# The last slot of a dense group: its eight narrow products first, then its wide ones tile by tile

## The chip, the cores and the metric

The kernel runs on one core of a Trainium2 chip. The metric is device time in microseconds (us) of one execution; the median of three runs is compared. Times inside the kernel come from one further execution, taken by the hardware profiler. Engines are named as the profile names them: PE (TensorE, matmuls), PEld (its weight loads), DVE (VectorE), ACT (ScalarE), POOL (GpSimd), SP (SyncE, which issues most DMAs).

## The reference

Two transformer blocks on 256 tokens of width 2048, in f32, with a final norm after each. What matters here is the order of the dense products:

```
first block:   p = rms_norm(x) @ w_in                      # 2048 -> 6000
               h = x + concat(rwkv7(p), sparse_attention(p)) @ w_mix_out
               h = h + cross_attention(rms_norm(h), rms_norm(mem))     # q, k, v, o
               h = h + square(relu(rms_norm(h) @ w_up)) @ w_down       # 2048 -> 8192 -> 2048
second block:  z = gelu(n @ a_w_in); u, v = split(z)                   # 2048 -> 2 x 4096
               h = h + gate * ((u * mix_tokens(rms_norm(v))) @ a_w_out)
               g, v = split(conv3(n @ ffn_w_up))                       # 2048 -> 2 x 5632
               h = h + gate * ((silu(g) * v) @ ffn_w_down)
```

## The kernel before

**Slots.** All dense weights come as one stream of 872 slots. A slot holds 256 rows by 512 columns of a weight matrix (512 KB) and lands by DMA in one of four ring places of `raw`. ACT copies it, rounded, to `whi` (L1933), DVE subtracts the two to `wlo` (L2282), and PE multiplies both. Semaphores keep the order: `hi_done` and `lo_done` count the two halves of a slot, and `slot_used`, raised by PE behind the last product that needs a slot, lets ACT write the ring place again.

**Wide and narrow products.** An operand is split in the same way, into a high part in columns 0 to 255 and a low part in columns 256 to 511 of `x`. A *wide* product multiplies `whi` with both (512 columns, L2742). A *narrow* one multiplies `wlo` with the high part alone (256 columns, L2746). Both add into one PSUM bank.

**Groups.** A dense group is 512 output columns: eight slots deep, four tiles of 128 columns wide, each tile in a bank of its own (two sets of four banks in turn). Each slot has two chunks `c` of 128 rows, so a slot is 8 wide and 8 narrow products. There are 64 such groups, all issued by `group()`: 12 in the first projection `w_in` (the last of them with three tiles), 4 in `mix_out`, 1 each for `k` and `q`, 16 in the first MLP (`mlp`), 8 in `a_uo`, and 22 in the conv FFN. The others, the down projections above all, go through `group_by_token` or `group_one_sum` and aren't touched.

Within a group, in `w_in` a slot's narrow products stand directly behind its wide ones. Elsewhere they stand in pairs: behind the wide ones of every second slot come the 16 narrow ones of both. The slot before the last has its narrow products alone. The last slot goes tile by tile: two narrow and two wide products of tile 0, then of tile 1, and so on, so that tiles are complete one after the other. `tile_done` tells of the first three, `slot_used` of the last.

**Asides.** Ahead of each slot's products a group may issue other PE work, `aside(g, s)`, with its own waits: index scores, `norm_k_t` (L1032), `bonus_t` (L1074) and `turn_t` (L1085 to L1089) of the mixer during `w_in`, `spread` (L2908) of the norm's factors in the first MLP group, `mixing` (L1802) in `a_uo`.

**Emptying a tile.** ACT's `half` (`hl`, L1940) waits for the tile and copies its upper 256 columns out of PSUM; DVE's `add` (L2307) adds the lower half to it and raises `evac_done`; further steps of the stage follow. `schedule()` puts the emptying of tile t on ACT and DVE behind the split of the t-th slot after the group's end, in one fixed order with the splits and with other work (L538, the ReLU of the index scores, stands on ACT behind the `half` of tile 0 of three groups in `w_in`). PE waits in some asides until all four tiles of a group are emptied (`evacuated(n)`: `evac_done` at 8 + 4n), or for a named step such as `rl2` or `rl5`, the ReLUs.

Of the kernel before, what the change touches and what calls it, by code (L numbers as in the profile page):

```python
# [1440 lines left out]
def build(nc, A, out):  # L1441
# [93 lines left out]
    L, n, g = {}, 0, 0  # L1535
# [1198 lines left out]
    def _(pe):  # L2734
        pe.sem_inc(slot_used, RING)

        def group(lin, i, g, x, ready, aside=None, tiles=4):

            p0, n = lin.ends[g] - lin.lens[g], lin.lens[g]

            def wide(s, c, t, stop=False):
                return pe.matmul(ps[:, lin.bank(g, t), :], whi[:, (p0 + s) % RING, c * 512 + t * P:c * 512 + (t + 1) * P],  # L2742
                                 x[:, 2 * s + c, :], start=s + c == 0, stop=stop)

            def narrow(s, c, t):
                return pe.matmul(ps[:, lin.bank(g, t), 0:T], wlo[:, (p0 + s) % RING, c * 512 + t * P:c * 512 + (t + 1) * P],  # L2746
                                 x[:, 2 * s + c, 0:T], start=False, stop=False)

            def narrows(s):
                pe.wait_ge(lo_done, lin.slot(i, p0 + s) + 1 + RING)  # L2750
                for c in range(2):
                    for t in range(tiles):
                        ins = narrow(s, c, t)
                ins.then_inc(slot_used, 1)

            for s in range(n - 1):
                if aside:
                    aside(g, s)
                begins = lin is L["w_in"] and (i, g, s) == (0, 0, 0)
                pe.wait_ge(*(hi_half, 1) if begins else (hi_done, lin.slot(i, p0 + s) + 1))  # L2760
                for c in range(2):
                    if begins and c:
                        pe.wait_ge(hi_done, 1)
                    if ready:
                        pe.wait_ge(ready[0], ready[1] + 2 * s + c + 1)
                    for t in range(tiles):
                        if s + c == 0:
                            pe.wait_ge(evac_done, lin.tile(i, g, t) + 1)
                        wide(s, c, t)
                if lin is not L["w_in"]:  # L2770
                    if s % 2:
                        narrows(s - 1)
                        narrows(s)
                    elif s == n - 2:
                        narrows(s)
                else:
                    narrows(s)
            s = n - 1
            if aside:
                aside(g, s)  # L2780
            pe.wait_ge(lo_done, lin.slot(i, p0 + s) + 1 + RING)
            if ready:
                pe.wait_ge(ready[0], ready[1] + 2 * n)
            for t in range(tiles):
                narrow(s, 0, t)
                narrow(s, 1, t)
                wide(s, 0, t)
                ins = wide(s, 1, t, True)
                if t < tiles - 1:
                    ins.then_inc(tile_done, 1 if t < tiles - 2 else 5 - tiles)  # L2790
            ins.then_inc(slot_used, 1)
# [75 lines left out]
        def run(nm, x, ready, aside=None):  # L2867
            lin = L[nm]

            def body(i, _):  # L2870
                for g in range(len(lin.lens)):
                    xx, rd = (x(g), ready(i, g)) if callable(x) else (x, ready)
                    group(lin, i, g, xx, rd, aside)
            for i in range(lin.iters):
                body(i, i == lin.iters - 1)
# [46 lines left out]
        lin = L["w_in"]  # L2922
# [12 lines left out]
        for i in range(lin.iters):  # L2935
            for g in range(2):
                group(lin, i, g, xn, (xn_ready, XP["mix"]) if i + g == 0 else None,
                      lambda g, s: beside_w_in(2 * i + g, s), min(4, NT - 8 * i - 4 * g))
# [14 lines left out]
        def cross_norm(g, s):  # L2953
            if (g, s) == (0, 5):
                stat("cross", L["q"].g0)
        group(L["k"], 0, 0, xn, (xn_ready, XP["mem"]), cross_norm)
        pe.wait_ge(rt_done, NORM["cross"] + 1)
        run("q", act_in, (xn_ready, XP["cross"]))
# [36 lines left out]
        lin = L["mlp"]  # L2995
# [11 lines left out]
        lin = L["a_v"]  # L3007
# [23 lines left out]
        for nm in ("ffn", "ffn_tail"):  # L3031
            lin, up = L[nm], TOKEN_DOWN[nm]
# [141 lines left out]
```

## Time and profile before

| | |
|---|---|
| median of three runs | 2651.3 us (2650.74 to 2651.79) |
| profiled execution: span | 2650.5 us, 0.8 us under that median |
| PE busy | 2622.0 us, 99% |
| weight loads busy | 2259.3 us, 85% (beside the matmuls) |
| DVE busy | 1931.6 us, 73% |
| ACT busy | 1381.8 us, 52% |
| mean granted TensorE clock | 0.999 |

The span is the time from the first to the last instruction of the profiled execution; no other time is measured for that execution. Busy shares are averages over stages that differ. In a timeline row, `[2.38 <-PE ps L2742]` says that the engine stood idle for 2.38 us before this instruction and that the product at line 2742 released it; equal neighbours are put together (`x10`), and a matmul's shown end is modelled, so distances are read from start to start.

### The profile page before, as it was taken

What the parts mean: (1) busy time and instruction counts of PE and PEld (TensorE: products, weight loads), DVE (VectorE), ACT (ScalarE), POOL (GpSimd) and SP (SyncE); (2) the same over time, 40 slices, a digit from 0 to 9 for tenths busy, and PEclk for the clock granted to TensorE, in tenths of its full rate; (3) what the DMA queues carried; (4) which work ended last, traced back from release to release, by engine and by line L of the source; (5) the groups of instructions that cost most, each with busy time, mean ns of one, the idle gap of its engine ahead of it and who ended that gap; (6) DMA issues with size and microseconds to landing.
All of it is one profiled execution on the core that took longest, in us unless ns stands there. A gap on an engine that the chain in (4) does not pass through costs nothing.

```text
span 2650.5 us, 46085 instructions
## 1 busy us (share of the span) xinstructions
PE 2622.0 (99%) x16930; PEld 2259.3 (85%) x16930; DVE 1931.6 (73%) x2963; ACT 1381.8 (52%) x2153; POOL 148.1 (6%) x162
## 2 busy tenths in 40 slices
PE   9999999999999999999999999999999999999998
PEld 8888888889888888888888888888888888888886
DVE  6778676877877877878887666578877756775676
ACT  6545555676544534435554454345455535553554
POOL 5600002301000000000000000000000000000000
PEclk9999999999999999999999999999999999999999
DMA  7555103555787787878778855677665555555554
GB/s 262 174 192 175 58 4 129 181 186 215 266 300 280 285 296 278 295 281 283 278 274 304 292 177 184 203 275 281 247 206 188 194 192 189 189 194 191 188 193 151
DMA packets 159504, 578.42 MB, mean 218 GB/s; under 512 B 18224, under 2 KB 18768, under 8 KB 158288
## 3 DMA queue, kind: packets, MB, share of 16 engines
q1 hardware_dynamic: 156224, 563.59, 61.3%
q10 hardware_dynamic: 2080, 9.46, 1.0%
q0 software_dynamic: 1008, 2.71, 0.4%
q8 instruction: 134, 2.20, 0.3%
q14 instruction: 58, 0.48, 0.1%
HBM read 572.81 MB, written 2.11 MB: 217 GB/s over the span
## 4 chain that ended last, share of the span: by engine, by line
PE 95%; DVE 2%; issue 1%; ACT 1%; POOL 1%; DMA 0%; SPq 0%; ACTq 0%; DVEq 0%; POOLq 0%
PE ps L2742 34%; PE ps L2746 18%; PE ps L2824 12%; PE ps L2826 12%; PE ps L2825 12%; PE ps L1151 1%; PE ps L1802 1%; PE ps L1164 0%; POOL ssm L1900 0%; DMA raw<-in_stream 0%; DVE wlo L2282 0%; PE ps L1100 0%; PE ps L2808 0%; PE ps L2809 0%; PE ps L2807 0%
## 5 line engine op out<-in xcount | busy, mean ns | idle before, releaser
L2282 DVE TENSOR_TENSOR wlo<-raw,whi 128x1024 fp32r<-128x1024 f32 x872 | 1059.3, 1230 | 516.8 <-ACT whi L1933 514.1
L1933 ACT ACTIVATE whi<-raw 128x1024 fp32r<-128x1024 f32 x871 | 903.3, 1056 | 778.7 <-PE ps L2746 367.9
L2742 PE MATMUL ps<-xn,whi 128*128 128x512 f32 x3760 | 941.3, 392 | 2.7 <-DVE wi L618 1.0
L2742 PEld LDWEIGHTS ps<-xn,whi 128*128 128x128 f32 x3760 | 674.7, 188 | 123.4 <-issue 2.2
L2746 PEld LDWEIGHTS ps<-xn,wlo 128*128 128x128 f32 x3760 | 510.8, 191 | 37.4 <-DVE wlo L2282 0.4
L2746 PE MATMUL ps<-xn,wlo 128*128 128x256 f32 x3760 | 520.6, 282 | 0.0
L2824 PE MATMUL ps<-whi,act_in 128*128 128x512 f32 x1120 | 436.1, 389 | 0.0
L2826 PE MATMUL ps<-whi,act_in 128*128 128x512 f32 x1120 | 435.7, 389 | 0.0
L2825 PE MATMUL ps<-wlo,act_in 128*128 128x512 f32 x1120 | 435.7, 389 | 0.0
L2824 PEld LDWEIGHTS ps<-whi,act_in 128*128 128x128 f32 x1120 | 210.2, 188 | 44.7 <-DVE wlo L2282 1.0
L2826 PEld LDWEIGHTS ps<-whi,act_in 128*128 128x128 f32 x1120 | 210.2, 188 | 43.7
L2825 PEld LDWEIGHTS ps<-wlo,act_in 128*128 128x128 f32 x1120 | 210.2, 188 | 43.5
L1940 ACT ACTIVATE hl<-ps 128x256 f32<-128x256 f32 x255 | 95.0, 373 | 130.5 <-PE ps L2742 130.4
L2824 PE MATMUL ps<-whi,xn 128*128 128x512 f32 x288 | 113.2, 393 | 0.7 <-issue 0.7
L2826 PE MATMUL ps<-whi,xn 128*128 128x512 f32 x288 | 112.2, 390 | 0.0
L2825 PE MATMUL ps<-wlo,xn 128*128 128x512 f32 x288 | 112.1, 389 | 0.0
L2742 PE MATMUL ps<-act_in,whi 128*128 128x512 f32 x320 | 80.4, 393 | 1.0 <-ACT whi L1933 1.0
L2742 PEld LDWEIGHTS ps<-act_in,whi 128*128 128x128 f32 x320 | 57.4, 188 | 12.0 <-ACT whi L1933 2.1
L2492 DVE TENSOR_TENSOR act_in<-tt,act_in 128x256 fp32r<-128x256 f32 x140 | 57.0, 420 | 11.7 <-ACT tt L2026 7.3
L2824 PEld LDWEIGHTS ps<-whi,xn 128*128 128x128 f32 x288 | 54.1, 188 | 12.5 <-issue 0.9
L2826 PEld LDWEIGHTS ps<-whi,xn 128*128 128x128 f32 x288 | 54.1, 188 | 11.4
L2825 PEld LDWEIGHTS ps<-wlo,xn 128*128 128x128 f32 x288 | 54.1, 188 | 11.1
(344 smaller groups left out, 2233.0 us busy)
## 6 DMA issues: line engine op xcount, KB each, us to landing
raw<-in_stream SPq DMA_DIRECT2D x872, 512.0 KB, 4.2
adaw<-in_ada SPq DMA_DIRECT2D x96, 512.0 KB, 5.8
adaq<-in_ada SPq DMA_DIRECT2D x96, 512.0 KB, 5.0
h<-in_xT SPq DMA_DIRECT2D x8, 256.0 KB, 8.9
memx<-in_memT ACTq DMA_DIRECT2D x1, 2048.0 KB, 9.2
gate_row<-gates POOLq DMA_DIRECT2D x2, 1024.0 KB, 7.6
lwa<-in_lora ACTq DMA_DIRECT2D x2, 512.0 KB, 4.5
lwa<-in_lora ACTq DMA_DIRECT2D x1, 1024.0 KB, 8.6
```

The source lines that it names most:

```text
L1151: ins = mm(ps[rows(1 - cc), 4 * g, u * HC:(u + 1) * HC], lm[g][rows(cc), hd, b, 0:CH], half_of(xx[g][rows(cc), 0, u, :], lv, 0), start=Tru ...
L1802: ins = pe.matmul(ps[:, mix_bank(k) + gr % 4, (2 * q + c) * P:(2 * q + c + 1) * P], vtk[:, gr, c, q * P:(q + 1) * P], wsr[c][:, gr, :], st ...
L1933: act.activation(whi[:, r, :], raw[:, r, :], ACT.Copy).then_inc(hi_done, 1)
L1940: act.activation(hl[:, t, :], ps[:, lin.bank(g, t), T:2 * T], ACT.Copy).then_inc(hl_done, 2 if last else 1)
L2282: dve.tensor_tensor(wlo[:, r, :], raw[:, r, :], whi[:, r, :].bitcast(F32), ALU.subtract)\
L2492: dve.tensor_tensor(act_in[:, m, T:2 * T], tt[:, m % 4, :], act_in[:, m, 0:T].bitcast(F32), ALU.subtract)\
L2742: return pe.matmul(ps[:, lin.bank(g, t), :], whi[:, (p0 + s) % RING, c * 512 + t * P:c * 512 + (t + 1) * P], x[:, 2 * s + c, :], start=s + ...
L2746: return pe.matmul(ps[:, lin.bank(g, t), 0:T], wlo[:, (p0 + s) % RING, c * 512 + t * P:c * 512 + (t + 1) * P], x[:, 2 * s + c, 0:T], start ...
L2824: pe.matmul(out, hi, whi[:, r, w], start=kc == 0, stop=False)
L2825: pe.matmul(out, hi, wlo[:, r, w], start=False, stop=False)
L2826: return pe.matmul(out, lo, whi[:, r, w], start=False, stop=kc == 2 * n - 1)
```

## The change

In the last slot of every dense group the order on PE becomes: the aside of the last slot, the narrow products of the slot before it, all eight narrow products of the last slot (chunk by chunk, all tiles), then the eight wide ones tile by tile, two for each tile. The narrow products of the slot before the last no longer stand ahead of that aside. Nothing is added or removed: the products, their operands, the waits and the semaphores raised are the same, in another order.

```diff
+            def after_pairs(s):
+                if lin is L["w_in"]:
+                    narrows(s)
+                elif s % 2:
+                    narrows(s - 1)
+                    narrows(s)
+
             for s in range(n - 1):
...
-                if lin is not L["w_in"]:
-                    if s % 2:
-                        narrows(s - 1)
-                        narrows(s)
-                    elif s == n - 2:
-                        narrows(s)
-                else:
-                    narrows(s)
+                if s < n - 2:
+                    after_pairs(s)
             s = n - 1
             if aside:
                 aside(g, s)
+            narrows(s - 1)
             pe.wait_ge(lo_done, lin.slot(i, p0 + s) + 1 + RING)
             if ready:
                 pe.wait_ge(ready[0], ready[1] + 2 * n)
+            for c in range(2):
+                for t in range(tiles):
+                    narrow(s, c, t)
             for t in range(tiles):
-                narrow(s, 0, t)
-                narrow(s, 1, t)
                 wide(s, 0, t)
                 ins = wide(s, 1, t, True)
                 if t < tiles - 1:
```

## Rows read from the trace of the kernel before

**Rows 1.** the page, head and part 1 (busy us, share, instructions)

```profile
span 2650.5 us, 46085 instructions
...
PE 2622.0 (99%) x16930; PEld 2259.3 (85%) x16930; DVE 1931.6 (73%) x2963; ACT 1381.8 (52%) x2153; POOL 148.1 (6%) x162
```

**Rows 2.** PE timeline, first MLP: start us, us, line, op, xcount [idle <-releaser]

```profile
1016.13 1.35 PE L2746 MATMUL ps<-xn,wlo 128*128 128x256 f32 x10
1017.33 0.63 PE L2742 MATMUL ps<-xn,whi 128*128 128x512 f32 x2
...
1018.02 0.62 PE L2742 MATMUL ps<-xn,whi 128*128 128x512 f32 x2
...
1019.42 4.25 PE L2742 MATMUL ps<-xn,whi 128*128 128x512 f32 x18
1023.51 2.08 PE L2746 MATMUL ps<-xn,wlo 128*128 128x256 f32 x16
1025.42 3.82 PE L2742 MATMUL ps<-xn,whi 128*128 128x512 f32 x16
1029.07 2.08 PE L2746 MATMUL ps<-xn,wlo 128*128 128x256 f32 x16
```

**Rows 3.** the waits: engine line <- releaser: us in total, times, longest

```profile
ACT hl L1940 <- PE ps L2742: 130.4, 58, 2.5
```

**Rows 4.** timeline, end of group 4 of the first projection

```profile
123.28 0.39 ACT L1940 ACTIVATE hl<-ps 128x256 f32<-128x256 f32 x1 [2.38 <-PE ps L2742]
...
123.56 1.51 ACT L538 ACTIVATE rel<-ps 128x768 f32<-128x768 f32 x2
...
125.12 1.69 PEld L2742 LDWEIGHTS ps<-xn,whi 128*128 128x128 f32 x8 [0.23 <-ACT rel L538]
```

**Rows 5.** timeline, end of group 5

```profile
150.32 1.69 PEld L2742 LDWEIGHTS ps<-xn,whi 128*128 128x128 f32 x8 [0.23 <-ACT rel L538]
```

**Rows 6.** timeline, end of group 6

```profile
173.28 0.81 ACT L538 ACTIVATE rel<-ps 128x768 f32<-128x768 f32 x1
...
174.31 2.12 PEld L2742 LDWEIGHTS ps<-xn,whi 128*128 128x128 f32 x10
```

**Rows 7.** timeline, from the end of group 8 to the sums of squared keys

```profile
218.51 0.42 DVE L2307 TENSOR_TENSOR proj<-ps,hl 128x256 f32<-128x256 f32 x1 [1.39 <-ACT hl L1940]
...
227.99 0.42 DVE L2307 TENSOR_TENSOR proj<-ps,hl 128x256 f32<-128x256 f32 x1
...
228.66 1.02 PE L1032 MATMUL ps<-blk,kq 128*128 128x2 f32 x8 [0.17 <-issue]
```

**Rows 8.** timeline, from the end of group 10 to the bonus sums

```profile
268.14 0.39 ACT L1940 ACTIVATE hl<-ps 128x256 f32<-128x256 f32 x1 [1.57 <-PE ps L2742]
...
275.30 0.42 DVE L2307 TENSOR_TENSOR proj<-ps,hl 128x256 f32<-128x256 f32 x1
...
275.77 1.13 PE L1074 MATMUL ps<-bp,blk 128*128 128x256 f32 x4 [1.41 <-DVE proj L2307]
```

**Rows 9.** timeline, before the second mixing step

```profile
1565.77 1.23 DVE L2282 TENSOR_TENSOR wlo<-raw,whi 128x1024 fp32r<-128x1024 f32 x1 [1.27 <-ACT whi L1933]
```

**Rows 10.** timeline, the conv FFN

```profile
1938.44 1.06 ACT L1933 ACTIVATE whi<-raw 128x1024 fp32r<-128x1024 f32 x1 [1.03 <-PE ps L2746]
```

**Rows 11.** timeline, end of group 0 of the first MLP

```profile
660.22 1.11 PE L2746 MATMUL ps<-xn,wlo 128*128 128x256 f32 x8
...
660.48 0.16 DVE L2347 SCALAR_TENSOR_TENSOR nt<-nt 128x2 f32<-128x2 f32 x1
...
661.16 0.38 PE L2908 MATMUL ps<-ident,nt 128*128 128x128 f32 x2
```

**Rows 12.** timeline, end of group 11 of the first projection

```profile
286.44 0.42 DVE L821 TENSOR_TENSOR ar<-proj,e 128x256 f32<-128x256 f32 x1
...
290.65 0.76 ACT L1940 ACTIVATE hl<-ps 128x256 f32<-128x256 f32 x2
```

**Rows 13.** the costliest groups: busy us, mean ns of one, idle before it

```profile
L2746 PEld LDWEIGHTS ps<-xn,wlo 128*128 128x128 f32 x3760 | 510.8, 191 | 37.4 <-DVE wlo L2282 0.4
```

## The prediction

> **What bounds the kernel now.** I read the page's head first. TensorE (PE) is busy for 2622.0 us of the 2650.5 us span, 99%, and VectorE (DVE) and ScalarE (ACT) have slack on the average [rows 1]. So the time is PE's matmul stream plus the few places where that stream stops. Two kinds of question follow: does the new order change the distance from matmul to matmul, and does it make PE stop longer somewhere?
>
> For the first I read PE's timeline over one group boundary of the first MLP [rows 2]. It shows the old end of a group (10 narrow products, 2 wide, then pairs, the last wide ones at the head of a run of 18) and, behind it, 16 narrow and 16 wide in two unbroken runs, which is what the end of a group becomes. For the second I read the table of waits. ACT's copy `hl` (L1940), the first step that empties a tile, waited for PE 58 times, 130.4 us in all, at most 2.5 us [rows 3]. That is nearly once for each of the 64 dense groups. ACT stands ready for tile 0, and whatever makes tile 0 later makes its `hl` later by the same. Then I followed each group end in the timeline until the lateness either met a wait on PE or ran into idle time of ACT or DVE.
>
> **The change, part by part.**
>
> *Order of the products.* No instruction is added or removed: the same 16 narrow and 8 wide ones close a group. Old, from the rows: from the first narrow to the start of the run of 18 wide ones 1019.42 − 1016.13 = 3.29 us, and the first two of that run still belong to the group. They cost (1023.51 − 1019.42)/18 = 0.227 us each, so 3.29 + 0.45 = 3.74 us. New, by the runs behind it: 16 narrow in 1025.42 − 1023.51 = 1.91 us (0.119 each), 8 wide at (1029.07 − 1025.42)/16 = 0.228, so 1.91 + 1.83 = 3.74 us [rows 2]. The rows are rounded to 0.01 us, and that much in each of 64 groups is 0.6 us: **0, between −0.6 and +0.6**.
>
> *When tiles are complete.* Before, tile 0's last wide product stood behind 2 of the last slot's narrow ones; now it stands behind all 8. Six narrow at 0.119 us make tile 0 later by 0.72 us, tile 1 by 0.48, tile 2 by 0.24, tile 3 by nothing. This costs only where tile 0's chain ends in a wait of PE. The places:
>
> *Place 1, groups 4 and 5 of the first projection.* The first product of the next group waits for two ReLUs (L538) which stand on ACT right behind the `hl` of tile 0. In the trace `hl` waited 2.38 us for PE, ran at 123.28, the ReLUs at 123.56 for 1.51 us, and PE's weight load at 125.12 was released by them after 0.23 us of waiting [rows 4]. All of it is a chain without slack, and PE is its end already. The twin one group later has the same figure, at 150.32 [rows 5]. Each pays the whole 0.72 us: **+1.44** (from 1.0, should PE's own queue hide 0.2 of each, to 1.44).
>
> *Place 2, group 6* has only one ReLU there, at 173.28 for 0.81 us, ending at 174.09. The next group's loads begin at 174.31 in one run of 10 without a stop [rows 6]. Two of the ten still belong to group 6; at 2.12/10 = 0.21 us for one, the third, which is the one that waits for the ReLU, begins at 174.73. The ReLU made late by 0.72 ends at 174.81: **+0.1** (0 to 0.3).
>
> *Place 3, group 8* to the sums of squared keys (L1032), which wait for all four tiles of that group. DVE's `add` of tile 0 waited 1.39 us for `hl` and ran at 218.51; from there DVE works without a break through weight subtractions and adds up to the `add` of tile 3, 227.99 to 228.41, and PE goes on at 228.66 [rows 7]. DVE has no idle time in which to catch up: **+0.72** (0.5 to 0.72).
>
> *Place 4, group 10* to the bonus sums (L1074): the same picture. `hl` at 268.14 had waited 1.57 us, the `add` of tile 3 runs from 275.30 to 275.72 at the end of an unbroken chain on DVE, and PE has already stood for 1.41 us when it is released at 275.77 [rows 8]: **+0.72** (0.5 to 0.72).
>
> At all other group ends the lateness is taken up by idle time. Tightest where a mixing step waits for all tiles of a group of the second block: behind tile 0's chain DVE still waits 1.27 us for `whi`, and `whi` waits for a slot that PE releases when it did before [rows 9]; 0.72 goes into the 1.27. In the conv FFN ACT waits 1.03 us in the same way [rows 10]. If that cover were gone, each mixing step (three) would cost up to 0.72.
>
> *The step ahead of the last slot.* The aside of the last slot used to stand behind the narrow products of the slot before it and now stands ahead of them, 8 × 0.119 = 0.95 us earlier, with its waits. What is queued behind it on PE are all 24 products that close the group. Three asides have something there; the one in the output projection of the mixer waits only for a step long past. In group 0 of the first MLP it is the transposition of the norm's factors (L2908), which waits for DVE's last step at 660.48 + 0.16 = 660.64. PE now reaches it at 660.22, where the narrow ones began; it was reached at 661.16 without a wait [rows 11]. So PE stops for 0.42 us and the release: **+0.5** (0, should DVE's chain end 0.4 earlier, to 0.95, the whole of the move). At the end of the first projection it is the transpositions of the mixer. Their last input from DVE ends at 286.44 + 0.42 = 286.86. The last group has three tiles, so they begin 6 × 0.119 = 0.71 us earlier than at present; those that need this input come behind those of the mixer's other half, after 286.86, so no wait. ACT's `hl` of tile 0 stands at 290.65 behind other copies, not behind PE [rows 12], which takes up most of tile 0's lateness (4 × 0.119 = 0.48 us here): **+0.1** (0 to 0.5).
>
> No DMA, no instruction of SP and none of POOL moves, and the slots of the ring are released after as many products as before, except in the groups with a moved aside.
>
> [...] Every narrow product loads its own weights, and such a load is shown with 191 ns [rows 13], longer than the 119 ns between two narrow ones in a run [rows 2]. So loads already overlap the products ahead of them, and a long run of narrow ones goes at no slower pace. [...]
>
> **Sum.** 0 + 1.44 + 0.1 + 0.72 + 0.72 + 0.5 + 0.1 = 3.6 us, by the bounds −0.6 + 1.0 + 0 + 0.5 + 0.5 + 0 + 0 = 1.4 to 0.6 + 1.44 + 0.3 + 0.72 + 0.72 + 0.95 + 0.5 = 5.2 us. The profiled span goes from 2650.5 to 2654.1. The median of the three runs, 2651.3, lies 0.8 us over that span, and I carry the 0.8 along: **2654.9 us**, 2652.7 to 2656.5 by the bounds. A measurement of this kernel tells about 0.2%, 5.3 us, from no change: below 2646.0 is faster, over 2656.6 slower. So this case is within it.
>
> **Rivals.**
>
> *Hidden.* The late tiles are caught up before PE asks, and only the moved aside costs: 2651.3 + 0.5 + 0.1 = 2651.9 us. For it: most group ends have more than 1 us of idle time on ACT and DVE. Against: in places 1, 3 and 4 PE waits in the trace already [rows 4, 5, 7, 8].
>
> *More chains are exposed.* The three mixing steps lose their cover: 3 × 0.72 = 2.2, so 2657.1 us, slower. For it: DVE has 1.27 us there at the tightest, and other work must not have moved into it. Decides when what is left of that wait is under 0. Against: 1.27 − 0.72 leaves 0.55 [rows 9].
>
> *Changes of kind cost PE time* (the faster side). Before, a group's end changes between narrow and wide 8 times, now twice. If a change cost 0.025 us, 6 × 64 of them would give back 9.6 us: 2654.9 − 9.6 = 2645.3 us. It decides from (3.6 + 5.3)/384 = 0.023 us. Against: two wide and two narrow take 1018.02 − 1017.33 = 0.69 us or, by the runs, 2 × 0.228 + 2 × 0.119 = 0.69 [rows 2]; so the cost is below about 0.005 us, 1.9 us in all.
>
> *Weight loads bind in the runs.* A narrow behind a narrow at 0.191 instead of 0.119 us; there are 15 such neighbours where there were 12, so 3 × 0.072 × 64 = 13.8 us: 2668.7 us. The measured run of 16 at 0.119 contradicts it [rows 2]. [...]
>
> **How the numbers follow.** The forecast 0.63, hidden 0.17, more exposed 0.13, changes of kind 0.04, weight loads 0.03. Faster holds only the changes of kind, 0.04; within 0.2% the forecast and the hidden case, 0.80; slower the other two, 0.16. The time is the forecast's, 2654.9. The forecast's own range is 2652.7 to 2656.5. The whole range runs from 2651.3 (hidden, with the low end of the pitch: 2651.9 − 0.6) to 2658.1 (more exposed, with the high ends of pitch and aside: 2657.1 + 0.6 + 0.45), and leaves out the last two cases and the tails.
>
> **What would show it.** In the profile after: a group's end as one run of 16 narrow and one of wide products in 3.74 us; `hl` of tile 0 after about 0.7 us more of waiting (58 × 0.7, so the group of 130.4 near 170); PE's wait before the products behind groups 4 and 5 near 0.95 us instead of 0.23, before L1074 near 2.1 instead of 1.41, about 0.9 before L1032; a wait of 0.4 to 0.5 us before L2908, where there was none. I am wrong if those stay as they are, or if the mixing steps or the FFN show a PE wait that was not there.

## The result and the profile after

The changed kernel takes 2657.55 us in the median of 21 runs (2653.94 to 2661.41), the kernel before beside it 2651.96 us (2650.29 to 2653.83). The ratio is 1.0022, interval 1.0016 to 1.0028: 5.8 us slower by that ratio, between 4.2 and 7.4 (5.6 by the two medians). That lies inside the range given, above the forecast of 2654.9 and above the 2656.6 from which a loss was to count as one. The span of the profiled execution is 2652.8 us, 2.3 us more than that of the one before. Both facts need explaining: where the 2.3 are, and why the median moved by more than twice that. Medians below leave out three slow executions of 3244 to 5287 us.

The page of the changed kernel, head and part 1:

```profile
span 2652.8 us, 46085 instructions
...
PE 2622.2 (99%) x16930; PEld 2260.3 (85%) x16930; DVE 1928.5 (73%) x2963; ACT 1380.5 (52%) x2153; POOL 150.4 (6%) x162
```

PE's busy time is the same to 0.2 us [rows 1]: nothing was added to the work. Where the loss is, the starts of the instructions have to say, since the shown ends of matmuls are modelled.

Its waits (engine, line, releaser: us in all, times, longest), those that answer to the steps of the prediction:

```profile
ACT hl L1940 <- PE ps L2742: 175.5, 61, 3.2
...
PE ps L1074 <- DVE proj L2307: 2.1, 1, 2.1
...
PE ps L2742 <- ACT rel L538: 1.0, 2, 0.5
...
PE ps L1032 <- DVE proj L2307: 0.9, 1, 0.9
...
PE ps L2911 <- DVE nt L2347: 0.3, 1, 0.3
```

ACT waits for tile 0 45 us longer than before, 0.7 for each of some 60 groups [rows 3], and it costs nothing in most of them. Four places show it on PE: the two ReLUs, L1032 and L1074. L2911 is the old L2908, the transposition with the moved aside.

Its timeline at the same places as in [rows 2, 4, 8, 11]:

```profile
124.00 0.39 ACT L1940 ACTIVATE hl<-ps 128x256 f32<-128x256 f32 x1 [3.10 <-PE ps L2742]
...
124.28 1.51 ACT L538 ACTIVATE rel<-ps 128x768 f32<-128x768 f32 x2
...
125.83 1.69 PEld L2742 LDWEIGHTS ps<-xn,whi 128*128 128x128 f32 x8 [0.93 <-ACT rel L538]
...
271.15 0.39 ACT L1940 ACTIVATE hl<-ps 128x256 f32<-128x256 f32 x1 [2.28 <-PE ps L2742]
...
278.78 1.13 PE L1074 MATMUL ps<-bp,blk 128*128 128x256 f32 x4 [2.13 <-DVE proj L2307]
...
661.94 0.16 DVE L2347 SCALAR_TENSOR_TENSOR nt<-nt 128x2 f32<-128x2 f32 x1
...
662.16 0.43 PE L2911 MATMUL ps<-ident,nt 128*128 128x128 f32 x2 [0.32 <-DVE nt L2347]
...
1018.18 2.08 PE L2746 MATMUL ps<-xn,wlo 128*128 128x256 f32 x16
1020.09 5.63 PE L2742 MATMUL ps<-xn,whi 128*128 128x512 f32 x24
1025.56 2.08 PE L2746 MATMUL ps<-xn,wlo 128*128 128x256 f32 x16
```

The reader is to see three things. The `hl` of tile 0 waits 0.72 us longer (3.10 for 2.38, 2.28 for 1.57), and the wait behind it on PE is longer by 0.70 and 0.72. At L2911 a wait of 0.32 us stands where there was none. And the group's end with the 16 wide products behind it takes 1025.56 − 1018.18 = 7.38 us, as it did in the old order (1023.51 − 1016.13, [rows 2]): in one group the order of the products is worth nothing that a row of 0.01 us can show.

Set side by side, the starts of the same instructions in the two profiled executions give the loss step by step (us; read from the two timelines):

```
                                   before   after    later by
scores in group 5 (L688)           133.71   134.42    0.71
scores in group 6 (L688)           158.90   160.32    1.42
transpositions in group 7 (L733)   183.24   184.78    1.54
sums of squared keys (L1032)       228.66   230.93    2.27
bonus sums (L1074)                 275.77   278.78    3.01
mixer's first products (L1115)     291.62   294.63    3.01
last L1223 of that chunk           395.86   397.18    1.32
cross-attention (L1727)            612.94   614.40    1.46
spread of the factors (L2908/11)   661.16   662.16    1.00
next transpositions (L2989/92)     675.29   677.29    2.00
end of the span                   2650.5   2652.8     2.3
```

Down to the mixer it is the forecast, step for step. That the two executions stand level before the first of these steps (0.0 us apart at 100 us) is in part chance. The changed kernel was 0.3 us late from the first 20 us on and then waited 0.4 us less for the index weights (`wi`, L618) behind group 3. That wait was in the profile of before, and the prediction did not price it. Before, then changed:

```profile
PE ps L2742 <- DVE wi L618: 1.0, 1, 1.0
...
PE ps L2742 <- DVE wi L618: 0.6, 1, 0.6
```

It is 0.60 to 0.63 us in all eight profiled executions with the new order in the first projection. In the six others it is 0.99 (before, experiment 1) or 0.22 to 0.25 us (experiments 4, 10, 11 and 12). So the new order can cost 0.4 us here as well as give 0.4 back. What decides it no experiment shows.

Then 1.7 us come back at 393 us, inside the mixer, which the change doesn't touch. The windows of the kernel before say why (us, PE busy, PEld, DVE, ACT, POOL, granted clock, DMA share, GB/s):

```profile
392.00:393.00 1.00, 0.13 (x8) 0.00 (x0) 0.78 (x5) 0.61 (x2) 0.00 (x0) 1.00 0.00 0
393.00:394.00 1.00, 0.79 (x6) 0.68 (x7) 0.97 (x5) 0.00 (x0) 0.00 (x0) 0.67 0.00 0
394.00:395.00 1.00, 1.00 (x7) 1.00 (x6) 1.00 (x5) 0.00 (x0) 0.00 (x0) 0.50 0.06 16
395.00:396.00 1.00, 1.00 (x7) 0.77 (x7) 0.34 (x2) 0.04 (x1) 0.00 (x0) 0.50 0.00 0
396.00:397.00 1.00, 0.83 (x13) 0.64 (x15) 0.50 (x2) 1.00 (x3) 0.00 (x0) 0.62 0.00 0
```

PE had stood still for 1.08 us (ahead of L1223 at 393.21), then the granted clock was 0.50 instead of 1.00 for 3.4 us, and PE lost 1.7 us (3.01 − 1.32 in the table). Apart from the last 4 to 6 us of each, the profiled execution of before had one such stretch and that of the changed kernel none. So 2.3 us is what the two executions differ by, and not the price of the change. Without that stretch the table gives 3.01 us up to the mixer and 2.00 − 1.46 = 0.54 at the moved aside, 3.5 in all. The last 0.3 us, from 2.00 to 2.3, come in bit by bit. From those transpositions to the last product of the last down projection it is 1965.5 to 1965.6 us in the five profiled executions with the old order there. With the new order it is 1965.8 to 1965.9 in seven of eight (1966.6 in experiment 5). So some 45 groups in the new order cost 0.3 us together, too little for a row of one of them. The comparison of the runs still says 5.8.

### The profile page after: what moved, and what is told of

It reads as the page before. It is cut to its first block, busy times and chain, and to the rows that moved or that the text cites. A ratio compares the mean times of both kernels' runs of the same rounds, so it can differ in the third digit from the quotient of the medians.

```text
span 2652.8 us, 46085 instructions
## 1 busy us (share of the span) xinstructions
PE 2622.2 (99%) x16930; PEld 2260.3 (85%) x16930; DVE 1928.5 (73%) x2963; ACT 1380.5 (52%) x2153; POOL 150.4 (6%) x162
## 4 chain that ended last, share of the span: by engine, by line
PE 95%; DVE 2%; issue 1%; ACT 1%; POOL 1%; DMA 0%; SPq 0%; ACTq 0%; DVEq 0%; POOLq 0%
PE ps L2742 33%; PE ps L2746 18%; PE ps L2827 12%; PE ps L2829 12%; PE ps L2828 12%; PE ps L1151 1%; PE ps L1802 1%; DVE wlo L2282 1%; PE ps L1164 0%; POOL ssm L1900 0%; PE ps L1100 0%; DMA raw<-in_stream 0%; PE ps L2811 0%; PE ps L2810 0%; PE ps L2812 0%
## 5 line engine op out<-in xcount | busy, mean ns | idle before, releaser
L2742 PE MATMUL ps<-xn,whi 128*128 128x512 f32 x3760 | 911.9, 392 | 3.5 <-ACT rel L538 1.0
L2742 PEld LDWEIGHTS ps<-xn,whi 128*128 128x128 f32 x3760 | 687.4, 188 | 139.2 <-issue 2.4
L2746 PEld LDWEIGHTS ps<-xn,wlo 128*128 128x128 f32 x3760 | 486.7, 191 | 21.3
L2746 PE MATMUL ps<-xn,wlo 128*128 128x256 f32 x3760 | 493.5, 283 | 0.0
L2307 DVE TENSOR_TENSOR zc<-ps,hl 128x256 f32<-128x256 f32 x88 | 37.0, 421 | 44.9 <-ACT hl L1940 44.9
L2307 DVE TENSOR_TENSOR tt<-ps,hl 128x256 f32<-128x256 f32 x112 | 46.9, 419 | 27.1 <-ACT hl L1940 25.6
L2827 PEld LDWEIGHTS ps<-whi,xn 128*128 128x128 f32 x288 | 54.1, 188 | 12.6 <-issue 0.9
```

What stands on the lines that cost most here:

```text
L2307: dve.tensor_tensor(dst, ps[:, lin.bank(g, t), 0:T], hl[:, t, :], ALU.add).then_inc(evac_done, count)
L2827: pe.matmul(out, hi, whi[:, r, w], start=kc == 0, stop=False)
```

## The experiments

Theory A: the loss is made of PE's waits in the first projection, 3.0 us, of the moved aside, 0.5, and, in many executions, of further stretches at half clock that follow the longer lulls. Theory B: what the traces don't show is spread over the other 52 groups. Each is compared with the kernel before on the same chip, and one execution of each was profiled.

**1. Old order in the first projection, new order elsewhere.**

```diff
+            new = lin is not L["w_in"]
+            if not new:
+                narrows(s - 1)
             if aside:
                 aside(g, s)
-            narrows(s - 1)
+            if new:
+                narrows(s - 1)
...
+                if not new:
+                    narrow(s, 0, t)
+                    narrow(s, 1, t)
                 wide(s, 0, t)
```

> New order in the 52 groups outside the first projection, old order in its 12. Theory A (the loss is made of waits in the first projection, 3.0 us by the traces, and of more stretches at the lower clock behind these longer waits, some 2 us; outside it only the moved aside costs, 0.5 us): +0.5 us over before, one wait of 0.3 to 0.5 us at the transposition of the norm's factors, none at the ReLUs beyond 0.23, 1.41 at the bonus sums. Theory B (the part of the loss that the profiled execution does not show comes from the 52 other groups, from later tiles or from the spacing of products): +2.5 us.

Measured 2651.25 us against 2651.33, ratio 1.0002 (0.9993 to 1.0011). Its waits:

```profile
PE ps L1074 <- DVE proj L2307: 1.4, 1, 1.4
...
PE ps L2919 <- DVE nt L2347: 0.3, 1, 0.3
```

The 52 groups with the new order cost nothing that the time can show, although tile 0 is late in each. The interval reaches +2.9 us, so this time alone does not shut out theory B's +2.5. The trace shows in those groups 0.6 us at the moved aside and the 0.3 us named above, and experiment 2 has the loss without them.

**2. New order in the first projection alone** (`new = lin is L["w_in"]` in the same edit).

> New order in the 12 groups of the first projection alone. Theory A: the waits at the ReLUs, at L1032 and L1074 as in the changed kernel (0.5 twice, 0.9, 2.1 us), +3.0 us of them, and with the lower clock behind them +5 us over before, with spans that differ more from run to run than those of before. Theory B: +3.0 us and no wider scatter than before.

2657.37 us against 2651.33, ratio 1.0018 (1.0009 to 1.0027); the runs lie between 2653.08 and 2659.95, those of before between 2649.72 and 2653.95. Twelve groups make the loss, as far as 2.4 to 7.2 us can tell, and the wide scatter too. Its profiled execution shows what the first one of the changed kernel did not. Timeline of PE and windows at the bonus sums:

```profile
278.34 1.32 PE L1074 MATMUL ps<-bp,blk 128*128 128x256 f32 x4 [2.13 <-DVE proj L2307]
279.12 3.10 PE L2742 MATMUL ps<-xn,whi 128*128 128x512 f32 x6
```

```profile
277.00:278.00 1.00, 0.00 (x0) 0.00 (x0) 1.00 (x2) 0.12 (x1) 0.00 (x0) 1.00 0.82 279
278.00:279.00 1.00, 0.66 (x3) 0.61 (x4) 0.97 (x3) 0.16 (x1) 0.00 (x0) 1.00 0.45 180
279.00:280.00 1.00, 1.00 (x5) 0.79 (x4) 0.63 (x2) 1.00 (x2) 0.00 (x0) 0.57 0.00 0
280.00:281.00 1.00, 1.00 (x4) 0.81 (x3) 0.58 (x1) 0.39 (x1) 0.00 (x0) 0.50 0.06 16
281.00:282.00 1.00, 1.00 (x3) 0.74 (x3) 0.65 (x1) 0.00 (x0) 0.00 (x0) 0.50 0.00 0
```

PE waits 2.13 us, as in the changed kernel, but then the clock is 0.50 and the six wide products, 1.73 us in the profiled execution of the changed kernel, take 3.10.

**3. The moved aside put back.**

```diff
+            narrows(s - 1)
             if aside:
                 aside(g, s)
-            narrows(s - 1)
```

> The changed kernel, only that the narrow products of the slot before the last stand ahead of the last aside again, as before the change. Both theories: the wait of 0.3 us at the transposition of the norm's factors is gone and 0.5 us come back there, all else as in the changed kernel: about +5 us over before. If the aside cost nothing, no difference to the changed kernel (+5.6).

2658.93 us, ratio 1.0024 (1.0015 to 1.0034): by the median no gain, and the interval cannot tell 5 from 7. The trace can: the wait at L2911 is gone, and from the cross-attention to the transpositions behind the first MLP's first group this execution gains 0.56 us on the changed kernel (4.93 us later than it at 614 us, 4.37 at 677). Its profiled execution has three stretches of 3.4 us at half clock, at 232, 280 and 447 us, which hide the half microsecond.

**4. Tile 0 earlier: the change mirrored.**

```diff
             s = n - 1
-            narrows(s - 1)
+            narrow(s - 1, 0, 0)
+            narrow(s - 1, 1, 0)
...
             for t in range(tiles):
+                if t == 1:
+                    for c in range(2):
+                        for u in range(1, tiles):
+                            ins = narrow(s - 1, c, u)
+                    ins.then_inc(slot_used, 1)
+                narrow(s, 0, t)
+                narrow(s, 1, t)
                 wide(s, 0, t)
```

(The eight narrow products of the last slot ahead of the loop go; the aside stands behind tile 0 outside the first projection.)

> The change mirrored: of the slot before the last, only tile 0's two narrow products stand ahead of tile 0's last four products, the other six behind them, so tile 0 is complete 0.72 us earlier than before, the others as before. Theory A: the waits at the ReLUs (0.23 twice) and at L1032 (0.17) go, that at L1074 falls from 1.41 to 0.7 us: 1.3 us less than before, or somewhat more if the clock falls less often. Theory B, or any in which tile 0's time is not what counts: no gain, 0 to +1.

2650.9 us against 2651.33, ratio 0.9999 (0.999 to 1.0008). The waits at the ReLUs and at L1032 are gone, as expected. That at L1074 fell only to 1.18 us:

```profile
265.86 0.38 ACT L1940 ACTIVATE hl<-ps 128x256 f32<-128x256 f32 x1 [0.84 <-PE ps L2742]
...
266.28 0.43 DVE L2307 TENSOR_TENSOR proj<-ps,hl 128x256 f32<-128x256 f32 x1
...
273.98 1.13 PE L1074 MATMUL ps<-bp,blk 128*128 128x256 f32 x4 [1.18 <-DVE proj L2307]
```

From the `hl` of tile 0 to the release are 273.98 − 265.86 = 8.12 us, before 275.77 − 268.14 = 7.63 [rows 8]. The chain got 0.5 us longer: the slot before the last is released later in this order, and the splits between the adds with it, which I had not counted. ACT's split waits 0.38 us for PE there and DVE's 0.55 us for ACT, where neither waited before:

```profile
266.62 1.06 ACT L1933 ACTIVATE whi<-raw 128x1024 fp32r<-128x1024 f32 x1 [0.38 <-PE ps L2746]
...
267.72 1.22 DVE L2282 TENSOR_TENSOR wlo<-raw,whi 128x1024 fp32r<-128x1024 f32 x1 [0.55 <-ACT whi L1933]
```

The order also has a price elsewhere that the expectation left out: a wait of PE for `wlo` (L2746), 0.38 us at 493 us in before, is 1.12 us here, since tile 0 asks for the last slot's low half earlier. That takes back 0.7 us, most of what the other waits gave. The waits moved as theory A has it; the time can't be told from no change.

**5. and 6. The waits filled.** PE gets dummy products in the two longer lulls, so that the wait costs what it did and PE is busy in it.

```diff
+            fill = {(9, 3): 8, (11, 2): 18}.get((g, s), 0)
+            if fill:
+                pe.wait_ge(evac_done, 8 + 4 * (g - 1) + 1)
+                for _ in range(fill):
+                    pe.matmul(ps[:, lin.bank(g - 1, 0), 0:P], ones[:, :], ones[:, :], start=True, stop=True)
             mixer["index_tensor"](pe, g, s)
```

> The changed kernel; 8 products of ones by ones (128 columns) are put ahead of the wait for the sums of squared keys (L1032), and 18 ahead of that for the bonus sums (L1074), into a bank that is already emptied; nothing reads them. PE's lulls of 0.89 and 2.13 us become busy, and what PE waits for comes no earlier. Theory A1 (the part of the loss beyond the waits is half clock that follows these lulls): no stretch at half clock between 200 and 300 us, the wait's own cost stays, so about 2655 us, 2 below the changed kernel. Rival A2 (the clock falls from run to run whatever happens at these two places): as the changed kernel, 2657.5.

2658.99 us, ratio 1.0029 (1.0018 to 1.0039): too many products. 18 were shown as 36 passes in 4.18 us, and PE went on at 280.45 instead of 278.78. With 9:

> As the run with filled waits, but 9 products of ones ahead of the bonus sums instead of 18: each is shown as two passes of 0.113 us, so 18 took 4.1 us where the lull had room for 2.3, and held PE up by 1.7 us; 9 take 2.0 us. Theory A1: PE goes on at L1032 and L1074 when it did in the changed kernel, no half clock between 200 and 300 us, the fastest runs as fast as those of the changed kernel (2654 us) and the median below it by 1 to 2.5 us (falls of 1.7 us each that no longer happen). Rival A2: median and scatter as the changed kernel run beside it.

2656.98 us (2655.92 to 2659.62), ratio 1.0021 (1.0013 to 1.003). PE's timeline:

```profile
227.85 1.11 PE L2746 MATMUL ps<-xn,wlo 128*128 128x256 f32 x8
228.80 1.95 PE L2941 MATMUL ps<-ones 128*128 128x128 f32 x16
230.58 0.95 PE L1032 MATMUL ps<-blk,kq 128*128 128x2 f32 x8
...
275.35 0.87 PE L2746 MATMUL ps<-xn,wlo 128*128 128x256 f32 x6
276.06 2.17 PE L2941 MATMUL ps<-ones 128*128 128x128 f32 x18
278.35 1.13 PE L1074 MATMUL ps<-bp,blk 128*128 128x256 f32 x4
279.13 1.74 PE L2742 MATMUL ps<-xn,whi 128*128 128x512 f32 x6
```

The same places in the changed kernel:

```profile
228.93 1.11 PE L2746 MATMUL ps<-xn,wlo 128*128 128x256 f32 x8
230.93 1.02 PE L1032 MATMUL ps<-blk,kq 128*128 128x2 f32 x8 [0.89 <-DVE proj L2307]
...
275.78 0.87 PE L2746 MATMUL ps<-xn,wlo 128*128 128x256 f32 x6
```

From the narrow products ahead of it to the bonus sums it is 278.35 − 275.35 = 3.00 us, as in the changed kernel (278.78 − 275.78): that lull is full, and the six wide products behind it take 1.74 us. Ahead of L1032 eight products are too many: 230.58 − 227.85 = 2.73 us against 230.93 − 228.93 = 2.00, so the filling itself holds PE up by 0.73 us.

The clock came as the theory says. There is no stretch at half clock between 200 and 300 us in either filled execution. The 11 runs lie within 3.7 us, where 21 of the changed kernel span 7.5. None of the 19 filled runs has a mean clock under 0.998, where 10 of 28 runs of the changed kernel have one. The mean over the 11 is 0.9984 against 0.9978, and 0.0006 of 2657 us is 1.5 us given back. The time came only in part. The 0.73 us take half of that 1.5 away, and the median is 0.4 us under that of the changed kernel beside it, which is not clear of the scatter. The fastest run is 2.0 us above the fastest of the changed kernel; 0.7 of that is the first filling. In the profiled execution PE also waits 1.77 us for `whi` at 480 us, behind ACT's squares of the memory, and that wait is 0.4 us or none in eleven others and 1.1 to 1.8 in two. Whether the filled runs have it more often stays open. So the filling shows that the clock came back, and does not show the full price in the time.

**7. The changed kernel once more**, beside the run with 9 products.

> The changed kernel once more, on the same chip as the run with 9 filling products. Theory A: about 2657.5 us again, its runs scattered over 5 us or more, and the profiled execution with none to three stretches of 3.4 us at half clock, each behind a lull (L1032, L1074, the mixer's L1223 or L1335).

2657.36 us, ratio 1.0024 (1.0013 to 1.0035). This execution has stretches of 3.41 us at half clock at 230.9 (behind the wait of 0.89 us at L1032), at 370.9 and at 446 us.

**8. Tile 0 later still.**

```diff
             for t in range(tiles):
                 wide(s, 0, t)
+            for t in range(tiles):
                 ins = wide(s, 1, t, True)
```

> The changed kernel with the eight wide products of the last slot chunk by chunk over all tiles, so that tile 0 is complete another three wide products (0.68 us) later, tile 1 by 0.46, tile 2 by 0.23. Theory A: each of the four waits grows by 0.68 us and the one ReLU of group 6 shows a wait of 0.6: 3.3 us above the changed kernel in the profile, 2661 us or more by the clock. If the waits were bounded by something else than tile 0's time: no more than 1 us above the changed kernel.

2661.71 us, ratio 1.0036 (1.0023 to 1.005); its waits:

```profile
PE ps L2742 <- ACT rel L538: 2.9, 3, 1.2
PE ps L1074 <- DVE proj L2307: 2.8, 1, 2.8
...
PE ps L1032 <- DVE proj L2307: 1.6, 1, 1.6
```

Every one of the four waits grew by 0.7 us, the third ReLU joined, and the mixer began 3.4 us later than in the changed kernel (298.03 for 294.63). At these places PE's waits followed tile 0's time one to one, 0.7 us for the 0.68 by which it was later.

**9. to 11. The three steps moved out of the way.**

```diff
-        for at_n, js in ((39, (0,)), (41, (1, 2)), (47, (3,)), (49, (4, 5)), (55, (6,)), (57, (7,))):
+        for at_n, js in ((39, (0,)), (40, (1, 2)), (47, (3,)), (48, (4, 5)), (55, (6,)), (56, (7,))):
             if n == at_n:
                 for j in js:
                     relu(j)
...
-        if (g, s) == (9, 3):
+        if (g, s) == (9, 4):
...
-        if (g, s) == (11, 2):
+        if (g, s) == (11, 3):
```

In the changed kernel:

> The changed kernel with three steps of the first projection moved so that late tiles meet no wait of PE: the sums of squared keys and what follows them one slot later (slot 4 of group 9), the bonus sums one slot later (slot 3 of group 11), and the ReLUs of groups 4, 5 and 6 on ACT one slot earlier, ahead of tile 0's copy. Theory A: the four waits (0.5, 0.5, 0.9, 2.1 us) and the half clock behind them go; of the change only the moved aside remains: before + 0.5 − 1.9 (what before itself waited there) = 2650 us. If the later steps are themselves waited for, that wait shows on PE up to group 11's end and in the mixer, and the gain falls short by it.

2650.72 us against 2651.32, ratio 0.9997 (0.9988 to 1.0006). All four waits are gone, and with them the loss. (The moves also take away what before itself waited there, so the next run is the one to compare with.) In the kernel before:

> The kernel before with the same three moves as in the run with later steps, and nothing of the change. Its waits of 0.23, 0.23, 0.17 and 1.41 us go: 2.0 us less than before, 2649.3 us, if no new wait comes. Against the changed kernel with the same moves it shows what the change costs where late tiles meet no wait: 0.5 us by theory A, 0 or less if the new order has an advantage of its own that the waits hid.

2648.98 us, ratio 0.9991 (0.9982 to 1.0). And again:

> The kernel before with the three moved steps once more, for a second interval: 2649 us, 2 to 2.5 us under before; if the first difference was chance, within 1 us of before.

2648.42 us against 2651.74, ratio 0.9989 (0.9981 to 0.9998). This is the fastest version found, 2.3 to 3.3 us under before. The new order costs 1.7 us against it even so (2650.72 to 2648.98 on one chip; 1.2 by the means), where 0.5 was forecast. The two profiled executions show 0.6 of it at the moved aside, 0.4 at the wait for the index weights (0.63 us for 0.24), and 0.3 spread over the groups behind; the rest can't be told from scatter.

**12. One longer wait by itself.** The kernel before, the bonus sums one slot earlier (`(11, 2)` to `(11, 1)`).

> The kernel before, with the bonus sums one slot earlier (slot 1 of group 11 instead of slot 2); nothing of the change. PE arrives there 2.1 us earlier and what it waits for comes when it did: the wait at L1074 grows from 1.41 to 3.5 us and nothing else moves. Theory A1 (a longer lull also brings stretches at half clock): fastest runs 2.1 us above the fastest of before, the median 3 to 4 us above, and a mean granted clock over the runs below before's 0.9987. Rival A2: median 2.1 us above before and the mean granted clock of before.

2654.43 us against 2652.09, ratio 1.0009 (1.0 to 1.0018). The wait is 3.52 us, and in its profiled execution the clock falls in it:

```profile
275.20 2.08 PE L1074 MATMUL ps<-bp,blk 128*128 128x256 f32 x4 [3.52 <-DVE proj L2307]
276.72 2.50 PE L2742 MATMUL ps<-xn,whi 128*128 128x512 f32 x6
```

```profile
274.00:275.00 1.00, 0.00 (x0) 0.00 (x0) 1.00 (x2) 0.00 (x0) 0.00 (x0) 0.97 0.91 319
275.00:276.00 1.00, 0.80 (x2) 0.71 (x3) 0.97 (x3) 0.30 (x1) 0.00 (x0) 0.50 0.35 139
276.00:277.00 1.00, 1.00 (x4) 0.80 (x3) 0.49 (x2) 0.30 (x1) 0.00 (x0) 0.50 0.00 0
```

The mean granted clock over its 11 runs is 0.9981, that of the 14 runs of before beside it 0.9986. That speaks for the lull; the median, 2.3 us above before, is hardly more than the 2.1 that the wait alone would give, so the price by the median is not settled here.

**What the runs add up to.** Over the 80 runs of before beside experiments 1 to 11 the mean granted clock is 0.9987, over 28 of the changed kernel 0.9978. 0.0009 of 2655 us is 2.4 us of clock lost, or 1.4 more stretches of 3.41 us at half clock in an average execution, 1.7 us each. With the 3.5 of the waits and the 0.3 spread over the later groups that makes 6.2 us, and 5.8 were measured, between 4.2 and 7.4. The runs of the changed kernel bear it out one by one: those with a mean clock of 0.999 took 2654.4 us on the mean (4 of them), with 0.998 2656.9 (14), with 0.997 2659.7 (10). That is 2.6 us for each 0.001, which is what 0.001 of 2655 us comes to. Which lulls it follows: of six profiled executions with 2.1 us or more unfilled at L1074, three have a stretch at half clock there (experiments 2, 3 and 12), and none of the three with 1.4 us or less (before, 1 and 4). Of five with 0.9 us or more at L1032, two (3 and 7). In the mixer, which the change doesn't touch, lie nine of the 14 stretches: five in the five executions that have the longer waits unfilled, four in the nine others. So at most the 0.8 per execution seen at L1032 and L1074 is traced to the longer waits; whether they also make the mixer's stretches more frequent, so few executions can't say. It doesn't come every time, and what decides it in one execution no run shows.

## Why the prediction was right in its mechanism and low in its price

*Order of the products, 0:* right within its ±0.6; 7.38 us both ways in one group, and 0.3 us in all over the groups behind the first MLP's first.

*Place 1, two ReLUs, +1.44:* 1.42 by the starts of L688. *Place 2, +0.1:* 0.12. *Place 3, +0.72:* 0.73. *Place 4, +0.72:* 0.74. The waits rose as forecast, 0.23 to 0.93 us at the weight loads, 1.41 to 2.13 at L1074, and to 0.89 at L1032. *The end of the first projection, +0.1:* 0.0. *The moved aside, +0.5:* a wait of 0.32 us shown at L2911, 0.54 by the starts behind it. Sum of the traces 3.5, forecast 3.6, with the 0.3 of the order 3.8.

*All other group ends, nothing:* right outside the first projection (experiment 1). Behind group 3 the prediction passed over PE's wait for the index weights, which the profile of before showed with 0.99 us; with the new order it is 0.6 us, in other executions of the old order 0.2. The mixing steps and the FFN show no new wait, so "more chains are exposed" is refuted, "hidden" by experiment 2, "weight loads bind" and "changes of kind" by the equal 7.38 us.

The step that failed is the *Sum*: it set each wait down at what it lasts and put the clock at nothing. In the traces a PE that had stood for 2.1 us or more at L1074 also came back at half clock for 3.4 us, in three of six executions, and behind the 0.9 us at L1032 in two of five. By the mean granted clock that added about 2.4 us to the average execution, two fifths of the loss, on top of waits that were sized to 0.1 us. About 1.4 of it (four stretches in five executions) stands in the traces at L1032 and L1074; where the rest falls is open. The profile before had a granted clock of 0.999 and one such stretch inside the mixer; I read the mean and not where it was lost. The listed runs also show the time 1.75 to 1.93 us above the span of the same execution, not the 0.8 that I carried along, so that the profiled execution of before, by that gap some 2652.3 us, probably stood 1 us above the 2651.3 of its median; its one stretch at half clock cost 1.7.

The chance of 0.80 for "within 0.2%" rested on the same omission: 3.6 us were under 5.3, and no case in the list joined the waits to the clock.

That the whole range, 2651.3 to 2658.1, still holds 2657.55 is luck. The forecast's own range ended at 2656.5, under the measured time. What reaches up to 2658.1 is the case of the three mixing steps, which showed no wait.

## What to carry to other kernels

PE was the bound here and its sequence dense (busy for 99% of the span), and what the reordering cost was found at the few places where a consumer already waited for the first tile: a lateness of 0.72 us there went on undiminished (0.71 to 0.74 us by the starts), and at nearly all other group ends it cost nothing. Price a longer stop of TensorE as its length plus a chance of a stretch at half clock (here 1.7 us, in three of six executions behind 2.1 us or more), and compare means of the granted clock over many runs before taking one profiled execution for the time. And if a wait is at the end of a chain without slack, move the waiting step and not the tile: here three moved steps were worth more than any order of the products that was tried.

## What the runs showed of the hardware

Every one of the 14 stretches at half clock (0.50) in the middle of these executions lasted 3.41 us, whether it came with a lull of 0.9 us (experiment 7, L1032) or of 3.5 us (experiment 12), and half of that, 1.7 us, is what each cost; the starts in the table show 1.69 for that of before. The same lull in the same program was followed by it in one execution and not in another: 0.89 us at L1032 in the changed kernel, a stretch at 230.9 us in experiment 7, none in its first profiled execution. The lull of 0.9 us was followed by another 0.9 us of products of two columns (L1032), so that it did not stand alone. With dummy products in the lulls no such stretch followed them in either profiled execution, and no run of 19 had a mean clock under 0.998, where 10 of 28 without them had; two of the five unfilled executions had none there either, so the count of the runs carries this and not the two traces.
